# The sample tokens' cached attention, divided by key/value head pair and computed inside the attention layer's group loop

## The reference

```python
def sink_attend(q, k, v, dist, valid, sinks, table):
    s = jnp.einsum('...qhgd,...khd->...hgqk', q, k).astype(jnp.float32) * (1.0 / math.sqrt(HEAD_DIM))
    s = s + rel_bias(dist, table)
    s = jnp.where(valid, s, NEG_INF)
    sk = sinks.astype(jnp.float32).reshape(N_KV_HEADS, GROUP, 1, 1)
    m = jnp.maximum(jnp.max(s, axis=-1, keepdims=True), sk)
    p = jnp.exp(s - m)
    p = p / (jnp.sum(p, axis=-1, keepdims=True) + jnp.exp(sk - m))
    o = jnp.einsum('...hgqk,...khd->...qhgd', p, v.astype(jnp.float32))
...
def cached_attention(q, k_new, v_new, k_past, v_past, sinks, table):
...
    k_all = jnp.concatenate([k_past.astype(k_new.dtype), k_new], axis=1)
    v_all = jnp.concatenate([v_past.astype(v_new.dtype), v_new], axis=1)
...
    valid = (dist >= 0) & (dist < WINDOW)
    return sink_attend(q, k_all, v_all, dist, valid[None, None], sinks, table)
...
# layer B: y = o * silu(gate);  x + rmsnorm(y @ w_out, g_post)
```

## Time and profile before

| | |
|---|---|
| median of 3 runs | 3246.95 us (3246.89 to 3247.03) |
| span of the profiled execution | 3245.9 us, mean granted PE clock 0.937 of full |
| PE busy | 2847.7 us (88% of the span) |
| GpSimd busy | 1625.3 us (50%) |
| DVE busy | 1139.6 us (35%) |
| ACT busy | 710.6 us (22%) |
| transfers | 245.4 MB, 76 GB/s over the span |
| chain of work that ended last | PE 77%, SP's transfer issues 6%, DVE 6%, GpSimd 4% |

### The profile page before, as it was taken

How to read it: one execution, slowest core, us unless ns; L and a number is a source line. 1 busy time by engine, 2 the same in 40 slices (tenths; PEclk the granted TensorE clock), 3 DMA queues, 4 the chain that set the end, 5 groups by cost and what they waited for, 6 DMA issues and landing times.

```text
span 3245.9 us, 51244 instructions
## 1 busy us (share of the span) xinstructions
PE 2847.7 (88%) x17686; PEld 2741.2 (84%) x17686; DVE 1139.6 (35%) x2670; ACT 710.6 (22%) x1671; POOL 1625.3 (50%) x2909
## 2 busy tenths in 40 slices
PE   4999999999998999779999999999999902599994
PEld 3999999999998999669889889988988802599993
DVE  4333343434343000383551654255245501100006
ACT  4023202311241010232331322133123201101103
POOL 2576687668753333585446455644655400133323
PEclk7999999999999999889999999999999955699996
DMA  8211111111141222721112111111111102322227
GB/s 247 88 56 52 42 55 58 52 48 52 55 140 49 75 71 65 279 108 45 43 40 64 37 50 54 45 50 43 60 42 43 45 28 71 119 66 73 65 97 252
DMA packets 302784, 245.38 MB, mean 76 GB/s; under 512 B 11978, under 2 KB 279466, under 8 KB 301515
## 3 DMA queue, kind: packets, MB, share of 16 engines
q1 hardware_dynamic: 250684, 180.38, 17.6%
q10 hardware_dynamic: 51944, 63.03, 5.6%
HBM read 184.54 MB, written 63.15 MB: 76 GB/s over the span
## 4 chain that ended last, share of the span: by engine, by line
PE 77%; SPq 6%; DVE 6%; POOL 4%; issue 4%; DMA 2%; ACT 1%; DVEq 0%; POOLq 0%; ACTq 0%
PE ps L498 67%; SPq L355 6%; PE ps L535 3%; PE ps L590 2%; PE ps L616 2%; POOL raw L402 2%; POOL wsp L406 2%; PE ps L603 2%; DMA x_t<-st 1%; ACT pt L926 1%; DVE xsp L1241 1%; DVE xsp L1104 1%; DVE rstd L1212 1%; DVE pp L1261 0%; DMA vc<-out_sample_v 0%
## 5 line engine op out<-in xcount | busy, mean ns | idle before, releaser
L498 PE MATMUL ps<-xsp,wsp 128*128 128x344 f32 x14976 | 2448.5, 324 | 114.3 <-POOL wsp L409 51.0
L498 PEld LDWEIGHTS ps<-xsp,wsp 128*128 128x128 f32 x14976 | 2387.7, 191 | 163.1 <-issue 73.8
L402 POOL TENSOR_SCALAR raw<-raw,prm 128x128 f32<-128x128 f32 x1152 | 459.2, 416 | 715.8 <-PE ps L498 609.6
L397 POOL CAST wsp<-raw 128x512 fp32r<-128x512 f32 x144 | 106.4, 739 | 689.6 <-PE ps L498 682.0
L406 POOL TENSOR_SCALAR wsp<-raw 128x128 fp32r<-128x128 f32 x1152 | 403.2, 375 | 56.4 <-POOL raw L402 56.4
L409 POOL TENSOR_TENSOR wsp<-raw,wsp 128x512 fp32r<-128x512 f32 x288 | 387.2, 1344 | 52.8 <-POOL wsp L406 52.8
L1199 DVE TENSOR_TENSOR acc<-acc,stg 128x1032 f32<-128x1032 f32 x32 | 39.5, 1235 | 664.0 <-ACT stg L848 664.0
L399 POOL TENSOR_TENSOR wsp<-raw,wsp 128x512 fp32r<-128x512 f32 x144 | 192.8, 1339 | 25.9 <-POOL wsp L397 25.9
L847 ACT ACTIVATE stg<-ps 128x344 f32<-128x344 f32 x96 | 45.3, 472 | 639.7 <-PE ps L498 639.7
L913 ACT ACTIVATE mx<-mx 128x2 f32<-128x2 f32 x128 | 26.1, 204 | 448.9 <-DVE mx L1267 448.9
L916 ACT ACTIVATE pp<-pp,mx 128x256 f32<-128x256 f32 (+1 forms) x256 | 122.9, 481 | 0.0
(11 more groups left out here) (193 smaller groups left out, 1957.0 us busy)
## 6 DMA issues: line engine op xcount, KB each, us to landing
raw<-in_a_w_in SPq DMA_DIRECT2D x128, 256.0 KB, 2.8
raw<-in_b_w_qg SPq DMA_DIRECT2D x128, 256.0 KB, 2.8
o_t<-stg ACTq DMA_DIRECT2D x32, 516.0 KB, 3.5
xsp<-o_t SPq DMA_DIRECT2D x8, 2064.0 KB, 12.8
raw<-in_a_w_out SPq DMA_DIRECT2D x64, 256.0 KB, 2.7
raw<-in_b_w_out SPq DMA_DIRECT2D x64, 256.0 KB, 2.7
xsp<-x_t SPq DMA_DIRECT2D x7, 2064.0 KB, 17.1
x_t<-stg ACTq DMA_DIRECT2D x16, 516.0 KB, 2.8
```

The source lines that it names most:

```text
L397: pool.tensor_copy(hi, w).then_inc(S["w_hi"], 1)
L402: op = pool.tensor_scalar(w[:, k], w[:, k], prm[:, k0 + k, gain:gain + 1], 1.0, ALU.mult, ALU.mult)
L498: op = pe.matmul(ps[:, b0 + g, 0:TG], wsp[:, slots[j], wh, k, :], xsp[:, kk, xh, grp(g)], start=(j == 0 and k == 0 and n == 0), stop=(j == ...
```

## The change

The sample attention's work for a pair of key/value heads (8 query heads, 8 sequences, so 64 rows of scores) is done in that pair's iteration of the group loop.

- **Tiles.** `kc`, `vc`, `sa`, `sbm`, `qbd`, `bsm` and `skp` are gone. The cached rows go to `kcv`, a view of the tile `k1`, keys first and then the values over them; the transposed keys `kst` are a view of `k2`. `k1` and `k2` hold the prompt's keys, last read by `scores` of the last block in slot 71. `pt` has one buffer and not two. New are `qz` (queries with zeros, written by `chunk_out` in place of `qs`), `sbias`, `sx` and `nsks`.
- **Transfers.** ACT issues them, and not SP: in `sample_keys` (slot 72) one transfer of 127 rows x 8 sequences x 128 columns, then one of the new rows; in `sample_turned` (slot 75) the same for the values. In chunk 5 SP loads the bias rows `sbias` with two small transfers. At the start SP loads the sinks as 4 columns of `nsks`, in place of `skp`.
- **PE.** 8 transposes at slot 75, 8 score products (of 64 rows by 128 cache rows, summed over the sequences, whose other rows are zero) at slot 77, one transpose of the probabilities at slot 79, 8 products with the values behind the last matmul of chunk 9.
- **Tail.** `out_phase` needs only the four reloads of `y_t`, which SP issues in the order 0 to 3 right behind the first weights, and `restage` of all four quarters stands ahead of the split of the sample columns (`smp_split`) that PE waits for.

```diff
-    kc = sb("kc", [P, 4, NB, P], where=z)
-    vc = sb("vc", [P, 4, NB, P], where=z)
...
+    kcv = k1[:, 0:SEQ].rearrange("p (b n) -> p b n", n=P)
+    kst = k2[:, 0:SEQ].rearrange("p (b n) -> p b n", n=P)
+    sp_, spT = kvo[0:HD, 0, :], kvo[:, 1, 0:HD]
...
-        sp.dma_start(skp[:], t["b_sinks"]).then_inc(S["tab_in"], 16)
+        for i in range(4):
+            sp.dma_start(nsks[:, i:i + 1], bass.AP(t["b_sinks"].tensor, i * NB, [[0, NB], [1, NB], [1, 1]]), allow_slow_non_contiguous=True)\
+                .then_inc(S["tab_in"], 16)
...
-        for cache, new, dst in ((t["cache_k"], t["sample_k"], kc), (t["cache_v"], t["sample_v"], vc)):
...
-                sp.dma_start(dst[1:P, :, b, :], cr[b, :, 1:P, :].rearrange("c r n -> r c n")).then_inc(there, 16)
-                sp.dma_start(dst[0:1, :, b, :], nr[b:b + 1]).then_inc(there, 16)
...
+        for kq in range(NQ):
+            lands(kq, Q_O2 - NQ, [(f"yb_out{m}", 32 * (kq + 1) + 16) for m in range(2)], [(1, y_t, SEQ)])
...
+        def sample_turn(i):
+            pe.wait_ge(S["o_read"], i * 32 + 33)
+            pe.wait_ge(S["pt_lo"], i * 32 + 33)
+            pe.wait_ge(S["smp_k_in"], i * 32 + 32)
+            for b in range(NB):
+                op = pe.transpose(ps[:, X0 + b // 4, (b % 4) * P:(b % 4 + 1) * P], kcv[:, b, :], ident[:])
+            op.then_inc(S["smp_pe"], 1)
...
+        def sample_mix(i):
+            pe.wait_ge(S["smp_act"], i * 4 + 4)
+            pe.wait_ge(S["smp_v_in"], i * 32 + 32)
...
+        def sample_keys(i):
+            act.wait_ge(S["s_read"], i * 32 + 33)
+            act.wait_ge(S["kv_out"], i * 64 + 128)
+            col = bass.ds(i * P, P)
+            act.dma_start(kcv[1:P, :, :], ck[1:P, :, col]).then_inc(S["smp_k_in"], 16)
+            act.dma_start(kcv[0:1, :, :], skn[:, :, col]).then_inc(S["smp_k_in"], 16)
+        def sample_turned(i):
+            act.wait_ge(S["smp_pe"], i * 4 + 1)
+            for n in range(2):
+                act.activation(kst[:, n * 4:n * 4 + 4, :].rearrange("p a b -> p (a b)"), ps[:, X0 + n, :], ACT.Copy)\
+                    .then_inc(S["smp_act"], 1)
+            col = bass.ds(i * P, P)
+            act.dma_start(kcv[1:P, :, :], cv_[1:P, :, col]).then_inc(S["smp_v_in"], 16)
+            act.dma_start(kcv[0:1, :, :], svn[:, :, col]).then_inc(S["smp_v_in"], 16)
...
+            todo += [(9 * 8, 0, lambda: sample_keys(i)), (9 * 8 + 3, 1, lambda: sample_turned(i)),
+                     (9 * 8 + 5, 1, lambda: sample_exp(i)), (9 * 8 + 7, 1, lambda: sample_probs(i))]
...
-        restage(64, SEQ, (1, 2))
...
+        restage(64, SEQ, range(NQ))
+            todo += [(9 * 8 + 5, 5, lambda: sample_max(i)), (9 * 8 + 6, 5, lambda: sample_scale(i)), (9 * 8 + 10, 5, lambda: sample_out(i))]
...
+        restage(32, SEQ, range(NQ))
         chunk_done(dve, C_O2 - 1)
         dve.tensor_copy(xsp[:, :, 0, SEQ:NT], qs[:, :, 0, :]).then_inc(S["smp_split"], 1)
```

More of the change, by code:

```diff
@@ L332, in group @@
                         .then_inc(S[f"b_in{j % 2}"], 16)
+                if c == 5:
+                    if not first:
+                        sp.wait_ge(S["smp_dve"], i * 3 - 2)
+                    for r0, n, j0 in ((1, P - 1, BLK), (0, 1, 2 * BLK - 1)):
+                        sp.dma_start(sbias[:, r0:r0 + n], bias_row[bass.ds(i * NB, NB), j0:j0 + n]
+                                     .rearrange("(o h) n -> o h n", o=1).to_broadcast([NB, NB, n]), allow_slow_non_contiguous=True).then_inc(S["smp_b_in"], 16)
                 if first and c == 0:
@@ L342, in _ @@
             group(i, False)
-        chunk(w_ob, 0, W_O2, O2_ORDER)
+        chunk(w_ob, 0, W_O2)
         for n in range(4):
             sp.wait_ge(S[f"x1_out{n}"], 80)
+        for kq in range(NQ):
+            lands(kq, Q_O2 - NQ, [(f"yb_out{m}", 32 * (kq + 1) + 16) for m in range(2)], [(1, y_t, SEQ)])
+        chunk(w_ob, P, W_O2 + NQ)
+        sp.wait_ge(S["smp_dve"], 3 * B_ITERS)
         sp.wait_ge(S["kv_out"], 64 * B_ITERS + 64)
-        sp.wait_ge(S["w_used"], Q_O2 - NQ + 1 + CREDIT)
-        for cache, new, dst in ((t["cache_k"], t["sample_k"], kc), (t["cache_v"], t["sample_v"], vc)):
[L350 to L353, removed]
-                sp.dma_start(dst[1:P, :, b, :], cr[b, :, 1:P, :].rearrange("c r n -> r c n")).then_inc(there, 16)
-                sp.dma_start(dst[0:1, :, b, :], nr[b:b + 1]).then_inc(there, 16)
[L356 to L364, removed]
         sp.dma_start(stg[:, 2:4, :, :].rearrange("p a b n -> p (a b) n"), x1_t[KT - QK:KT, :, :].rearrange("k p n -> p k n"))\
@@ L614, in mix @@
                 v = vn[:, b - 1 + kt, j // 2].rearrange("p v d -> p (v d)")
[L615 removed]
+                for part, p in enumerate((pt[:, :, :], ptl[:, :, :])):
                     op = pe.matmul(ps[:, X1, 0:2 * BLK], v, p[:, :, kt * P:(kt + 1) * P],
@@ L1383, in _ @@
-        own.link(dve.tensor_scalar(sx[:, 1, :], sx[:, 0, :], -1.0, None, ALU.mult))
-        dve.tensor_tensor(sx[:, 2, :], sx[:, 5, :], sx[:, 1, :], ALU.add).then_inc(S["smp_dve"], 1)
-        dve.wait_ge(S["smp_act"], 9)
-        own.link(dve.tensor_tensor(sx[:, 5, :], sx[:, 3, :], sx[:, 4, :], ALU.add))
-        own.link(dve.reciprocal(sx[:, 5, :], sx[:, 5, :]))
-        for n in range(2):
-            op = dve.tensor_scalar(sbm[:, n, :], sbm[:, n, :], sx[:, 5, n:n + 1], None, ALU.mult)
-        op.then_inc(S["smp_dve"], 1)
@@ L1408, in _ @@
         clear_acc()
-        restage(40, SEQ, (3, 0))
         out_phase(C_O2, 1)
```

216 lines of the change are left out of this document (78 added, 138 removed).

## The result

| | before | after |
|---|---|---|
| median, us | 3246.92 (4 runs, 3245.34 to 3247.03) | 3280.32 (4 runs, 3277.93 to 3290.69) |
| ratio | 1 | 1.011, 95% interval 1.0094 to 1.0126 |
| span of the profiled run, us | 3245.9 | 3288.8 (its time 3290.69) |

The change makes the kernel 1.1% slower. The forecast was 3265, slower; the time lies in the range of 3205 to 3305 and inside the forecast's own, 3248 to 3285.

What follows compares the result with a forecast made beforehand. PE was taken to bound the loop, with one-engine cache transfers holding their issuer. 3245.9 - 204.2 + 190.8 + 10 + 20.8 + 0.6 = 3263.9, with 1.05 around it 3265 us; range 3205 to 3305, the forecast's own 3248 to 3285.

Steps and rivals of the forecast that it cites:

- What goes, and the bound: PE's own work bounds the loop; the hole behind it, where PE waits during cached-row transfers, goes whole: -204.2 us.
- The issuer is held: At each group's cache transfers, ACT stands while one DMA engine takes them: 24.0 us for keys, 25.8 for values.
- the last part: Signs expected in the changed profile, among them eight new-row transfers on ACT's queue at some 23 us each.
- 47.7 us a group: Chunk 9 of each group ends later by key delay (23.8 us), value hold and products; 190.8 us for four.
- my 0.5 us for half clock left over: Part of each group's added time: PE still at half clock after the second stall, 0.5 us.
- The last group: Reloads of `y_t` land beside its keys and values on the shared engine: +10 us.
- The tail: Behind the last value products, PE waits for DVE's 16 restaging tiles, then the gate and split: +20.8 us.
- The start: Three more transfer issues ahead of the prompt's first rows, +1.2 us, less 0.6 of bias work: +0.6 us.
- Nothing for the plain chunks: The eight plain stretches between the stalls, over four groups, were taken as unmoved: 0 us.
- ACT isn't held: Rival: ACT's queue takes both transfers at once, so only PE waits for landings; 3215 us, chance 0.14.
- All 16 engines: Rival: the new cache transfers are spread, landing in 3 to 5 us, 9 us a group; 3100 us, chance 0.06.
- Sharing is dearer: Rival: weights and reloads take an even engine share, or clock costs 3 us a stall; 3297 us, chance 0.12.

Runs made afterwards that it cites:

- e5: The changed kernel with VectorE's split of the sample tokens' result put ahead of the 16 restaging operations at the loop's end: 3268.94 us, ratio 1.007.
- e10: The changed kernel with each block's two small 128x2 softmax operations on VectorE rewritten to read one SBUF tensor and a scalar pointer: 3275.91 us, ratio 1.0087.
- e11: e6 with the two small VectorE softmax operations rewritten to read one SBUF tensor each: 3081.63 us, ratio 0.9483 to the kernel before.
- e1: The changed kernel with each pair's small new-row transfer issued ahead of the 127 cached rows, keys and values: 3255.55 us, ratio 1.0032 to the kernel before.
- e3: The changed kernel with each transfer of 127 cached rows cut in 112 and 15, ACT still issuing: 3103.99 us, ratio 0.9564 to the kernel before.
- e6: The changed kernel with 127-row transfers cut in 112 and 15 and the split ahead of the restaging: 3093.21 us, ratio 0.9519 to the kernel before.

## Why the prediction was right, and where its sizes were off

**What goes, and the bound: right.** The hole of 204.2 us is gone, and PE was what counted in the loop: each hold came back nearly whole as PE's idle time (23.5 us of 25.0 behind the keys in the third group).

**The issuer is held: right, a little dearer.** Forecast 24.0 us for the keys and 25.8 for the values, made from SP's pairs; measured in the first three groups 25.0 to 25.5 and 27.2 to 27.3 for the second issue, and 25.4 to 25.9 and 27.6 for the pair, which is what was forecast. The eight rows on ACT's queue were "some 23 us" in the last part and are longer.

**47.7 us a group: mis-sized by 2.5.** Measured 49.9, 50.6 and 49.9. In the third group, counted from the chunk's start: `mix` of block 6 begins at 30.8 us for a forecast 29.3; the values' hold begins at 41.8 for 41.5 and ends at 69.1 for 67.3; the products end at 76.3 for 73.8. The two terms behind that are the pair of the values (27.6 us for 25.8) and its end: I let the products begin 3.0 us behind it, by ACT's chain, but the data came later, 3.7 us behind, so the chain was hidden behind the landing. A third is the clock. No row showed my 0.5 us for half clock left over by the second stall; the next chunk 0 measured 24.56 us for 22.93, which is 1.6 (the granted clock is 0.50 until 2472.8 us, and 1.00 from 2474.8). Against them PE had stood 0.9 us between the two chunks before and stands 0.4 now. Two sums of the prediction are off by 0.1 us: 22.0 and 1.7 are 23.7, and the tail's terms add up to 20.9.

**The last group: the right mechanism, 3.1 us too cheap.** Its holds are 30.5 and 34.8 us, 12.7 more than in the other groups, and its products end 13.1 later in the chunk, where the reloads of `y_t` on the same engine had been put at 10.

**The tail: right.** 20.8 us forecast; 20.1 of idle time measured behind the products, released by the split, and e5 shows that it was VectorE's order. That the wait could be had away for 11.4 us the prediction did not say.

**The start: a load mis-priced, but 0.4 us off in the end.** Four small loads of the sinks take 2.65 us on SP, 0.66 each, in place of one of 0.29; I had priced three more at 0.29 to 0.42, by loads of other shapes. The prompt's first rows are issued 2.4 us later for it (8.78 for 6.41 us). Of the +3.3 us in the table only 1.0 is left one chunk into the loop.

**Nothing for the plain chunks: wrong in this run.** +9.6 us there, +12.0 without the loop's first chunk. The prediction took the loop's other chunks as unmoved. They hold the same instructions, but stalls elsewhere moved the phase of VectorE against GpSimd, and twice as many operations met a lock. This is the largest single part of what the forecast lacked, and e10 and e11 show the mechanism. For the median of after it is smaller, since its other runs are 8 to 13 us faster than the profiled one; how many were held in those no trace shows. The direction does not rest on them: without any, e10 still took 3275.91 us.

**The rivals.** "ACT isn't held" fell by the rows of L933, and e1 showed that even so it would have come out at some 3255, not 3215: its landings, 25.6 and 28 us, were 4.4 and 2.4 too short, and those of the last group more. "All 16 engines" was 3100, and e3, which makes it true, gave 3103.99. "Sharing is dearer" was right only in the last group.

## To carry to other kernels

Before moving a transfer, look at how many DMA engines it has (its GB/s against a spread one's): here the shape, 127 rows, cost 176 us in the changed kernel and 139 in the one before, and the place alone, with spread transfers, 3.6. Taking a wait off the issuer helps only by what lies between the hold's end and the landing; a queue's next issue takes the hold over. Where two engines are in near lockstep, a step that "moves nothing" can still change which of them gets there first, and more so the more often they meet: 15 held operations cost the kernel before nothing to be seen, e6, with 42 in its profiled run, lost 11.6 us. Give small VectorE operations one SBUF tensor and a scalar pointer where GpSimd works beside them.

## What the runs showed of the hardware that I had not expected

- An issue of 4 KB stands for 25.0 to 34.8 us behind one of 508 KB on one DMA engine, while the large one's own issue takes 0.3. Put first, the small one takes 0.7 us, and the hold goes to the queue's next transfer: 16.7 us for a 512 KB store, 27.0 in the last group. It is the same on SP (24.8 us).
- PE can use the data of such a pair 3.7 us after the hold has ended, in all four groups (2466.93 for 2463.20 in the third). In e1, where the large transfer stands alone, it is 3.5 us after the next issue is let go (2406.07 for 2402.59).
- VectorE operations of 0.16 us are stretched to 1.0 to 1.3 us, to the end of a GpSimd operation, when they read two SBUF tensors and start 10 to 300 ns behind it, in either form tried. At the same 10 ns or ahead of it, or with one SBUF tensor, they are not; where VectorE's is ahead, GpSimd's takes 1.32 us for 1.29.
